# One transformer layer on one core: expert weights stored with even columns first, three stages run without borders between blocks, and the state-space setup staged a turn ahead

## The chip, the cores and the metric

The kernel runs on one core of a Trainium2 chip. The metric is the device time of one execution in microseconds; several executions are taken, and their median stands for the kernel.

## The reference, cut to what matters

One decoder layer with 1024 positions of width 1024, everything in fp32. A token mixer (a state-space branch beside dilated window attention) is followed by a residual and a LayerNorm, then by a mixture of 64 small experts, 8 of them for each position, and a shared one, and by a second residual and LayerNorm.

```python
def token_mixer(x, w_in, b_in, ...):
    proj = x @ w_in + b_in
    u, q, k, v, g_ssm, g_attn = jnp.split(proj, SPLIT_POINTS, axis=-1)
    y_ssm = s5_branch(u, lam_re, lam_im, log_dt, b_re, b_im, c_re, c_im, d_skip, w_glu) @ w_br_ssm
...
    merged = jax.nn.sigmoid(g_ssm) * y_ssm + jax.nn.sigmoid(g_attn) * y_attn
    return merged @ w_out

def swiglu(x, w_gate, w_up, w_down):
    return (jax.nn.silu(x @ w_gate) * (x @ w_up)) @ w_down
...
    def expert_block(acc, blk):
        e, rows, g = blk
        yb = swiglu(x2[rows], w_gate[e], w_up[e], w_down[e])
        return acc.at[rows].add(yb * g[:, None].astype(x2.dtype)), None
```

An expert has gate and up weights of 1024 x 256 and down weights of 256 x 1024, 3 MB together in fp32. The state-space branch (`s5_branch`) has 32 groups of 16 channels with 64 complex states each.

## The kernel before, in words

The program is a row of blocks. In each block every engine has its own stream of instructions, ordered by semaphores, and at a block's end all engines wait for each other; the setup of a block's semaphores and buffers stands there too. The blocks that matter here are these.

**`mixer_input`** transposes x, projects u (`ps_u`), works out the parameters of the state-space branch, and ends in a loop of TURNS = 8 turns over four groups each:

- ScalarE's `order` copies four groups of u (`u_tok`) into the buffer `u_stage`, in runs of 16 floats. VectorE's `stage` forms four products `w_prod` (L666) and combines them into `w_stage` (L672). Both buffers are single; `stage` of turn it waits for `turned`, the end of the transposes of the turn before.
- TensorE waits for `staged` and `ordered`, transposes four pieces of `u_stage` (L529) and four of `w_stage` (L531) into PSUM, makes the response products `ps_k` (L538, 16 instructions), waits for the copies of the transposes, and makes the states `ps_v` (L548, 16 instructions).
- ScalarE waits for `turned`, runs `order` for the next turn, copies the transposes into `ut_stage` (L602) and `wt_stage`, and then the responses into `k_resp`.
- GpSimd copies `ut_stage` on into `ut_all` (L473; the trace shows `ut_all` as part of `merged`). VectorE's `keep_states` copies `ps_v` into `keep["states"]`, behind `stage` of the next turn.

**`attention`** begins on TensorE with 16 steps of projection (`pe_project`, from L90, `mm3`: three fp32r products of high and low parts for one fp32 product). The first four steps fill one PSUM bank (`ps_p[:, 0]`), the fifth begins the second, where the states of the setup stood. Later lines that the rows show are L1239, L1040 and L1014, products of the attention's end with operands that lie next to each other.

**`project_and_route`** makes the output projection, LayerNorm, the router and the shared expert, whose last `down` on TensorE and `add_share` on VectorE end the block. It also asks for the first experts' weights and for the rows of the first items.

**`experts`** works on a list of 66 items, each a run of up to 160 positions of one expert. They are sorted by count into width classes, WIDTHS = (160, 144, 128, 112, 96); in the traced execution 12 items have width 160, 24 have 144, 14 have 128, 10 have 112 and 6 have 96. One turn does one item; the turns go in pairs with two sets of buffers (j = 0, 1). On TensorE a turn is: sums for the index of the item after next (L1816, L1818); 64 gate and up instructions (L2600: 2 matrices, 2 column halves c, 8 pieces k of the inner dimension; each fp32 product is two instructions in the trace); `turn_rows`, the transposes of the next item's rows (L2579, L2584); at widths over 128 the remaining rows' down product (L2614); and the down product as `mm3` (L90 to L92). The weights' stationary operand of L2600 is

```python
w3(raw[j][w])[:, k, c:2 * P:2]
```

that is, 128 columns, every second float of a run of 256, because hidden unit 2p + c is to stand on partition p: the down weights are loaded with two neighbouring rows on one partition. ScalarE makes, in this order, the high part of the next item's down weights (`split_hi`, L2642), SiLU, half of the next rows' copies, and the outputs. VectorE makes the low part of the down weights (`split_lo`, L2693) behind each piece of the high part, and the hidden values (`hidden`). SyncE asks for the weights of the item two turns ahead, with one transfer of 1024 KB for each of gate, up and down, when the buffers of the set come free. GpSimd gathers the rows of an item from `scr_x` (L1792) and adds the outputs to `scr_acc` (L2556). Ahead of the loop, TensorE runs `turn_rows(0)`; ScalarE runs `rows_in(0)` and `split_hi(0)`, and in its first turn `split_hi(1)` before item 0's SiLU.

Of the kernel before, what the change touches and what calls it, by code (L numbers as in the profile page):

```python
# [23 lines left out]
P = 128  # L24
D = 1024
# [277 lines left out]
def mixer_input(nc, m, cst, io, xT_hi, xT_lo, keep, scr, first):  # L303
# [5 lines left out]
    with ExitStack() as stack:  # L309
# [30 lines left out]
        ut_stage = a.sb("ut_stage", [P, 4, P])  # L340
# [6 lines left out]
        ld_x = [a.sem(f"ld_x{j}") for j in range(NT)]  # L347
        ld_dt, dt_ready, ld_lam, lam_copied = (a.sem(n) for n in ("ld_dt", "dt_ready", "ld_lam", "lam_copied"))
        ld_w = [a.sem(f"ld_uw{j}") for j in range(RAW)]
        ld_par, ld_bias = a.sem("ld_par"), a.sem("ld_bias")  # L350
        x_turned, x_hi_made, x_lo_made = a.sem("x_turned"), a.sem("x_hi_made"), a.sem("x_lo_made")
        p_turned, p_copied = a.sem("p_turned"), a.sem("p_copied")
        w_hi_made, w_lo_made, w_used = a.sem("uw_hi_made"), a.sem("uw_lo_made"), a.sem("uw_used")
        u_done, u_evac = a.sem("u_done"), a.sem("u_evac")
        den_ready, rden_ready, fac_ready, pow_ready, par_ready = (a.sem(n) for n in ("den_ready", "rden_ready", "fac_ready", "pow_ready", "par_ready"))
        pool_ch, dve_ch = a.sem("mi_pool_ch"), a.sem("mi_dve_ch")
        cpow_ready, zero_ready = a.sem("cpow_ready"), a.sem("zero_ready")
        ordered = a.sem("s5_ordered")
        staged, turned, copied_u, copied_w = a.sem("s5_staged"), a.sem("s5_turned"), a.sem("s5_ut"), a.sem("s5_wt")
        k_done, k_copied, v_done, v_copied = a.sem("s5_k"), a.sem("s5_kc"), a.sem("s5_v"), a.sem("s5_vc")  # L360
        ut_kept, stored, kd_ready = a.sem("s5_ut_kept"), a.sem("mi_stored"), a.sem("kd_ready")
# [5 lines left out]
        ps_ut = ps_u[:, 0].rearrange("p a (b c) -> p (a b) c", b=2)  # L367
        ps_wt = ps_u[:, 1].rearrange("p a (b c) -> p a b c", b=2)
# [48 lines left out]
        with nc.Block() as block:  # L417
            @block.sync
            def _(sp):
                def load_w(n):  # L420
                    if n >= RAW:
                        sp.wait_ge(w_lo_made, n - RAW + 1)
                    sp.dma_start(w_raw[:, n % RAW, :], w_d[:, n % KD, 0:SSM_W]).then_inc(ld_w[n % RAW], 16)

                for s in range(NT):
                    sp.dma_start(x_tok[:, s, :], x_d[:, s, :]).then_inc(ld_x[s], 16)
                    if 2 <= s < 2 + RAW:
                        load_w(s - 2)
                for n in range(RAW, 2 * RAW - 1):
                    load_w(n)  # L430
                for j, n in enumerate(("ssm_b_re", "ssm_b_im")):
                    sp.dma_start(b_raw[:, j, :, :], io[n][0].rearrange("(a g) n c -> (g n) a c", g=2)).then_inc(ld_par, 16)
                for j, n in enumerate(("ssm_c_re", "ssm_c_im")):
                    for half in range(2):
                        for g in range(2):
                            sp.dma_start(c_rows[:, j, half, SSM_N * g:SSM_N * g + SSM_N],
                                         io[n][0, 16 * half + g:16 * half + 16:2].rearrange("a c n -> a c n")).then_inc(ld_par, 16)
                sp.dma_start(d_row[:, :, :], io["ssm_d"].rearrange("o g c -> o (g c)").broadcast_to((SSM_C, SSM_G * SSM_C))
                             .rearrange("p (g c) -> p g c", c=SSM_C)).then_inc(ld_par, 16)
                sp.dma_start(bias_u[:, :], b_row[:, 0:SSM_W].broadcast_to((P, SSM_W))).then_inc(ld_bias, 16)  # L440
                for n in range(2 * RAW - 1, 2 * KD):
                    load_w(n)
                sp.wait_ge(w_lo_made, 2 * KD)
                first.load(sp)

                sp.wait_ge(zero_ready, 1)
                sp.dma_start(scr["k_pad"][:, :, 0:KP0], zeros[0:SSM_C, 0:KP0].unsqueeze(1).broadcast_to((SSM_C, SSM_G, KP0))).then_inc(stored, 16)
                for g2 in range(2):
                    rows = slice(64 * g2, 64 * g2 + 64)
                    sp.dma_start(scr["c_op"][rows, :, P * (1 - g2):P * (1 - g2) + P], zeros[rows, :].unsqueeze(1).broadcast_to((64, 2 * PAIRS, P))  # L450
                                 ).then_inc(stored, 16)
                sp.wait_ge(cpow_ready, 1)
                for g2 in range(2):
                    rows = slice(64 * g2, 64 * g2 + 64)
                    sp.dma_start(scr["c_op"][rows, :, P * g2:P * g2 + P],
                                 c_pow[rows, :, :, 1:T + 1, :].rearrange("p r a t c -> p (r a) (t c)")).then_inc(stored, 16)
# [20 lines left out]
            def _(pe):  # L477
# [22 lines left out]
                for n in range(2 * KD):  # L500
# [5 lines left out]
                    for s in range(4 * half, 4 * half + 4):  # L506
                        if half and k == 0:
                            pe.wait_ge(u_evac, s - 3)
# [2378 lines left out]
```

## Time and profile before

| what | value |
|---|---|
| median of 3 runs | 2113.94 us (2113.0 to 2120.82) |
| profiled execution | 2118.44 us, its span 2116.7 us |
| mean clock granted to TensorE | 0.977 |
| TensorE (PE) busy | 1997.8 us, 94% |
| its weight loads (PEld) | 1735.7 us, 82% |
| VectorE (DVE), ScalarE (ACT), GpSimd (POOL) busy | 1132.1, 771.5, 540.9 us |
| gate and up products, L2600 | 4224 instructions, 536.3 us |
| data moved | 390.19 MB, mean 184 GB/s |

The profiled execution is another one than the three timed runs; its own time lies 4.5 us above their median. The span is what the rows are placed in, in microseconds from its start. The setup loop runs up to 112 us, the attention block follows, and the experts' loop stands from about 1224 to 2084 us. TensorE is busy nearly all the time, so its share says little: whether it runs at its own pace, and where it stands still, has to be read from single stretches.

### The profile page before, as it was taken

The numbers are of one execution on the slowest core, as the hardware profiler recorded it, in microseconds if no ns is written. First come the engines' busy times: TensorE is split into PE (matmuls) and PEld (weight loads), VectorE is DVE, ScalarE is ACT, GpSimd is POOL, SyncE is SP. The second block draws the span as 40 slices with busy tenths as digits, with TensorE's granted clock in tenths as the row PEclk, the third lists the DMA queues.
The fourth block names the chain that finished last, engine by engine and source line by source line (L and its number), as shares of the span: only waits on it lengthen the run. The fifth ranks groups of instructions, "written<-read, shape, count | busy, mean of one in ns | idle before, by whom it ended". The sixth has DMA issues, their size and how long they took to land. (4 is left out here: it accounts for less than half of the span.)

```text
span 2116.7 us, 39190 instructions
## 1 busy us (share of the span) xinstructions
PE 1997.8 (94%) x12849; PEld 1735.7 (82%) x12849; DVE 1132.1 (53%) x3379; ACT 771.5 (36%) x1517; POOL 540.9 (26%) x969
## 2 busy tenths in 40 slices
PE   7889999999999889999899989999999999999992
PEld 7768889888988778888687778898888889999991
DVE  5833664456356652222556755555555556666654
ACT  4322453355144431111434023333333333333334
POOL 7145555200022300000100223334444332222120
PEclk9999999999999999999999999999999999999996
DMA  5522132211234521110341489999999999999995
GB/s 165 129 50 75 46 86 66 65 46 46 70 109 125 139 60 41 49 55 5 125 158 67 161 294 319 313 307 314 317 321 325 316 312 369 371 356 339 345 342 174
DMA packets 181200, 390.19 MB, mean 184 GB/s; under 512 B 26553, under 2 KB 121149, under 8 KB 155510
## 3 DMA queue, kind: packets, MB, share of 16 engines
q1 hardware_dynamic: 155568, 317.52, 41.7%
q0 software_dynamic: 25376, 71.46, 15.3%
q8 instruction: 52, 0.85, 0.2%
q14 instruction: 38, 0.31, 0.0%
q10 hardware_dynamic: 166, 0.05, 0.0%
HBM read 330.94 MB, written 64.98 MB: 187 GB/s over the span
## 5 line engine op out<-in xcount | busy, mean ns | idle before, releaser
L2600 PE MATMUL ps_gu<-xe,w_raw 128*128 128x144 f32 (+4 forms) x4224 | 536.3, 288 | 0.0
L2600 PEld LDWEIGHTS ps_gu<-xe,w_raw 128*128 128x128 f32 x4224 | 524.8, 197 | 0.2
L2642 ACT ACTIVATE w_hi<-w_raw 128x1024 fp32r<-128x1024 f32 x132 | 132.1, 1048 | 161.5 <-DMA w_raw<-in_exp_w_down 161.5
L2693 DVE TENSOR_TENSOR w_lo<-w_raw,w_hi 128x1024 fp32r<-128x1024 f32 x132 | 155.5, 1218 | 64.4 <-ACT w_hi L2642 64.3
L2556 POOL DMA_INDIRECT scr_acc<-y_main,out_idx x66 | 102.5, 1553 | 309.1 <-ACT y_main L2671 288.8
L1141 ACT ACTIVATE w_raw_first<-w_raw_first,o_stage 128x128 f32<-128x128 f32 (+1 forms) x192 | 86.4, 450 | 200.1 <-DVE o_stage L1089 199.2
L2671 ACT ACTIVATE y_main<-ps_ye,gate 128x512 f32<-128x512 f32 (+2 forms) x132 | 90.8, 688 | 123.5 <-PE ps_ye L92 123.5
L2647 ACT ACTIVATE xe<-ps_gu 128x512 f32<-128x512 f32 (+2 forms) x66 | 38.4, 581 | 216.2 <-PE ps_gu L2579 216.2
L2551 POOL DMA_INDIRECT scr_acc<-y_rest,out_idx x36 | 58.2, 1617 | 226.3 <-ACT y_rest L2668 226.3
L90 PE MATMUL ps_ye<-w_hi,e_h_hi 128*128 128x512 f32 (+2 forms) x264 | 109.9, 416 | 0.8 <-DVE e_h_lo L2720 0.7
L1808 DVE TENSOR_SCALAR e_sel<-e_slots,e_place 128x256 bf16<-128x256 bf16 (+1 forms) x536 | 104.6, 272 | 0.0
L92 PE MATMUL ps_ye<-w_hi,e_h_lo 128*128 128x512 f32 (+2 forms) x264 | 103.5, 392 | 0.0
L91 PE MATMUL ps_ye<-w_lo,e_h_hi 128*128 128x512 f32 (+2 forms) x264 | 103.4, 392 | 0.0
L1792 POOL DMA_INDIRECT x_main<-scr_x,idx x66 | 73.1, 1107 | 77.0 <-issue 47.9
L1827 DVE TENSOR_TENSOR e_idx_f<-ps_xt,e_neg_slot 128x2 f32<-128x2 f32 x64 | 10.2, 159 | 147.6 <-PE ps_xt L1818 122.2
L1040 PEld LDWEIGHTS ps_mixer<-merged,w_raw_first 128*128 128x128 f32 x560 | 78.4, 193 | 10.2 <-ACT w_raw_first L1150 1.7
L1040 PE MATMUL ps_mixer<-merged,w_raw_first 128*128 128x64 f32 x560 | 85.7, 261 | 1.1 <-DVE w_raw_first L1097 1.1
L90 PE MATMUL ps_mixer<-v_w_hi,xT_hi 128*128 128x512 f32 x192 | 80.5, 419 | 6.1 <-DVE v_w_lo L860 4.0
L90 PE MATMUL ps_mixer<-xT_hi,w_hi_first 128*128 128x512 f32 x192 | 79.4, 414 | 5.2 <-PEq L105 5.2
L1102 DVE COPY o_stage<-ps_mixer 128x64 f32<-128x64 f32 x192 | 42.4, 221 | 76.5 <-PE ps_mixer L1040 76.2
L1299 POOL TENSOR_TENSOR o_stage<-o_stage,att_wts 128x512 f32<-128x512 f32 x8 | 8.8, 1098 | 289.4 <-DVE att_wts L1289 289.4
L860 DVE TENSOR_TENSOR v_w_lo<-v_w_raw,v_w_hi 128x512 fp32r<-128x512 f32 x48 | 33.6, 702 | 87.4 <-ACT v_w_hi L856 87.3
(460 smaller groups left out, 4774.3 us busy)
## 6 DMA issues: line engine op xcount, KB each, us to landing
w_raw<-in_exp_w_gate SPq DMA_DIRECT2D x66, 1024.0 KB, 8.2
w_raw<-in_exp_w_up SPq DMA_DIRECT2D x66, 1024.0 KB, 7.4
w_raw<-in_exp_w_down SPq DMA_DIRECT2D x66, 1024.0 KB, 8.1
w_raw_first<-in_w_in SPq DMA_DIRECT2D x24, 512.0 KB, 4.4
v_w_raw<-in_w_in SPq DMA_DIRECT2D x48, 256.0 KB, 2.7
merged<-in_x SPq DMA_DIRECT2D x14, 512.0 KB, 5.0
scr_att<-o_stage SPq DMA_DIRECT2D x16, 264.0 KB, 3.0
att_prev<-scr_att SPq DMA_DIRECT2D x16, 264.0 KB, 3.4
```

Source lines behind the costliest of these rows:

```text
L90: eng.matmul(out, lh, rh, start=first, stop=False, skip_group_check=True)
L91: eng.matmul(out, lh, rl, start=False, stop=False, skip_group_check=True)
L92: return eng.matmul(out, ll, rh, start=False, stop=last, skip_group_check=True)
L1040: ins = pe.matmul(ps_o[:, w % 2, 0:DH], probs_T[:, w % 2, P * j:P * j + P], v_cur[:, kb, P * hp + DH * h2:P * hp + DH * h2 + DH], start=(j ...
L1141: act.activation(probs[:, w % 2, 0:n], probs[:, w % 2, 0:n], ACT.Exp, scale=-1.0, bias=o_stage[:, blk, at + 1:at + 2], accum_out=o_stage[: ...
L1792: pool.indirect_dma_start(out=self.x_main[j][0:rows, :], out_offset=None, in_=self.x_rows[0], in_offset=bass.IndirectOffsetOnAxis(ap=self. ...
L1808: ins = dve.tensor_scalar(self.sel[:, s, 0:slots], self.slots[:, 0:slots], self.place[:, s:s + 1], None, ALU.is_equal)
L2556: pool.indirect_dma_start(out=acc_rows[0], out_offset=bass.IndirectOffsetOnAxis(ap=out_idx[j][0:rows, 0:1], axis=0), in_=y_main[j][0:rows, ...
L2600: ins = pe.matmul(ps_gu[:, 2 * w + c, 0:width], w3(raw[j][w])[:, k, c:2 * P:2], xT[:, k, 0:width], start=(k == 0), stop=(k == KD - 1))
L2642: act.activation(piece_of(hi[j], piece), piece_of(raw[j][DOWN], piece), ACT.Copy).then_inc(hi_made, 1)
L2671: act.activation(y_main[j][0:rows, 512 * half:512 * half + 512], ps_y[0:rows, half, :], ACT.Copy, scale=gate[j][0:rows, 0:1]).then_inc(y_e ...
L2693: tt(piece_of(lo[j], piece), piece_of(raw[j][DOWN], piece), piece_of(hi[j], piece).bitcast(F32), ALU.subtract).then_inc(lo_made, 1)
```

## The change

Four edits. Most of the diff's length is indentation; it is shown here without it.

**Expert weights.** Before the launch, the host stores the columns of `exp_w_gate` and `exp_w_up` with the 128 even ones first and the 128 odd ones behind them. The kernel reads half c as a run of 128 neighbouring columns.

```diff
     for name, value in inputs.items():
         arr = np.ascontiguousarray(value)
+        if name in ("exp_w_gate", "exp_w_up"):
+            arr = np.ascontiguousarray(arr.reshape(1, NE, D, P, 2).swapaxes(3, 4)).reshape(arr.shape)
...
-                                ins = pe.matmul(ps_gu[:, 2 * w + c, 0:width], w3(raw[j][w])[:, k, c:2 * P:2], xT[:, k, 0:width],
+                                ins = pe.matmul(ps_gu[:, 2 * w + c, 0:width], w3(raw[j][w])[:, k, P * c:P * c + P], xT[:, k, 0:width],
                                                 start=(k == 0), stop=(k == KD - 1))
```

**The border before the attention.** `mixer_input` no longer has a block. It returns one function for each engine, and the attention block calls them at its head. Its semaphores come from the outer memory `m`. At their ends GpSimd, ScalarE and VectorE wait for the setup's stores, and GpSimd and VectorE for the last states too; TensorE waits for the states ahead of its fifth projection step.

```diff
-        with nc.Block() as block:
-            @block.sync
-            def _(sp):
+        def opening_sync(sp):
...
+            pool.wait_ge(ordered, TURNS)
+            pool.wait_ge(k_done, TURNS)
+            pool.wait_ge(v_copied, TURNS)
+            pool.wait_ge(stored, 16 * 5)
...
+            dve.wait_ge(stored, 16 * 5)
+            dve.wait_ge(v_copied, TURNS)
+
+        return opening_sync, opening_tensor, opening_scalar, opening_vector, opening_pool
...
             def _(sp):
+                opening_sync(sp)
                 sp_load_bias(sp, 0)
...
             def _(pe):
+                opening_tensor(pe)
                 for step in range(16):
+                    if step == 4:
+                        pe.wait_ge(first.states_kept, SSM_G // 4)
                     pe_project(pe, step, 0)
```

**The border before the experts.** `project_and_route` likewise returns `routing_sync` and its four sisters, which the experts' block calls at the head of each engine's stream.

```diff
             def _(pe):
+                routing_tensor(pe)
+
                 def turn_rows(j, uses, width):
...
+                pe.wait_ge(it.shares, NT - 1)
+                pe.wait_ge(it.idx_made, 2)
                 turn_rows(0, 1, CAP)
+                pe.wait_ge(it.shares, NT)
                 kinds, rest_pairs, pairs = classes(pe)
```

**The setup loop.** TensorE transposes turn it + 1 before it does the products of turn it, with two PSUM targets in turn. ScalarE copies the transposed u straight into `ut_all`; `ut_stage` and GpSimd's copy are gone. `order` moves from ScalarE to GpSimd, `keep_states` from VectorE to ScalarE, and ScalarE's and GpSimd's loops are written out.

```diff
-        ps_ut = ps_u[:, 0].rearrange("p a (b c) -> p (a b) c", b=2)
-        ps_wt = ps_u[:, 1].rearrange("p a (b c) -> p a b c", b=2)
+        ps_ut = [ps_u[:, 0].rearrange("p a (b c) -> p (a b) c", b=2), ps_x[:, 2, :].rearrange("p (g c) -> p g c", g=4)]
+        ps_wt = [ps_u[:, 1].rearrange("p a (b c) -> p a b c", b=2), ps_x[:, 3, :].rearrange("p (a b c) -> p a b c", a=2, b=2)]
+        ut_of = lambda it: keep["ut_all"][:, 512 * it:512 * it + 512].rearrange("p (g c) -> p g c", g=4)
...
-                with pool.Fori(0, TURNS) as it:
-                    pool.wait_ge(copied_u, it + 1)
-                    pool.tensor_copy(keep["ut_all"][:, bass.ds(it * 512, 512)],
-                                     ut_stage[:, :, :].rearrange("p a b -> p (a b)")).then_inc(ut_kept, 1)
+            for it in range(TURNS):
+                if it == 0:
+                    pool.wait_ge(u_evac, NT)
+                else:
+                    pool.wait_ge(turned, it)
+                pool.tensor_copy(u_stage[:, :, :].rearrange("p g (s c) -> p g s c", s=T),
+                                 u_tok[:, :, 64 * it:64 * it + 64].rearrange("p s (g c) -> p g s c", g=4)).then_inc(ordered, 1)
...
-                for it in range(TURNS):
+            def turn_stage(it):
                     pe.wait_ge(staged, it + 1)
                     pe.wait_ge(ordered, it + 1)
+                if it >= 2:
+                    pe.wait_ge(copied_w, it - 1)
                     for g in range(4):
-                        pe.transpose(ps_ut[:, g, :], u_stage[:, g, :], ident[:, :])
+                    pe.transpose(ps_ut[it % 2][:, g, :], u_stage[:, g, :], ident[:, :])
                     for j in range(4):
-                        ins = pe.transpose(ps_wt[:, j // 2, j % 2, :], w_stage[:, j // 2, j % 2, :], ident[:, :])
+                    ins = pe.transpose(ps_wt[it % 2][:, j // 2, j % 2, :], w_stage[:, j // 2, j % 2, :], ident[:, :])
                     ins.then_inc(turned, 1)
+
+            turn_stage(0)
+            for it in range(TURNS):
+                if it + 1 < TURNS:
+                    turn_stage(it + 1)
+                if it:
                     pe.wait_ge(k_copied, it)
...
+            def keep_states(it):
+                act.wait_ge(v_done, it + 1)
+                act.activation(keep["states"][:, :, 2 * it:2 * it + 2, 1:NCH + 1],
+                               ps_v.rearrange("p a r k -> p r a k"), ACT.Copy).then_inc(v_copied, 1)
 
-                def responses(it, more):
+            def responses(it):
                     act.wait_ge(turned, it + 1)
-                    if more:
-                        order(it + 1)
-                    act.wait_ge(ut_kept, it)
-                    act.wait_ge(v_done, it)
-                    act.activation(ut_stage[:, :, :], ps_ut, ACT.Copy).then_inc(copied_u, 1)
-                    act.activation(wt_stage[:, :, :, :], ps_wt, ACT.Copy).then_inc(copied_w, 1)
+                act.activation(ut_of(it), ps_ut[it % 2], ACT.Copy).then_inc(copied_u, 1)
+                if it:
+                    keep_states(it - 1)
+                act.activation(wt_stage[:, :, :, :], ps_wt[it % 2], ACT.Copy).then_inc(copied_w, 1)
                     act.wait_ge(k_done, it + 1)
```

## Rows read from the trace of the kernel before

**Rows 1.** Timeline, TensorE, gate and up streams of three turns: start, length (us), instructions
```profile
1706.63 8.09 PE L2600 MATMUL ps_gu<-xe,w_raw 128*128 128x144 f32 x64
...
1792.38 7.78 PE L2600 MATMUL ps_gu<-xe,w_raw 128*128 128x128 f32 x64
...
2020.64 7.76 PE L2600 MATMUL ps_gu<-xe,w_raw 128*128 128x96 f32 x64
```

**Rows 2.** Timeline, TensorE and its weight loads, 596.4 to 597.6 us
```profile
596.63 0.61 PE L1239 MATMUL ps_mixer<-v_w_raw,merged 128*128 128x128 f32 x4
...
597.07 0.30 PEld L1040 LDWEIGHTS ps_mixer<-merged,w_raw_first 128*128 128x128 f32 x2
...
597.29 0.19 PEld L1014 LDWEIGHTS ps_mixer<-k_two,q_two 128*128 128x128 f32 x1
```

**Rows 3.** Windows: us, busy PE PEld DVE ACT POOL, clock, DMA share, GB/s
```profile
1758.00:1884.00 126.00, 126.00 (x1021) 118.71 (x1017) 79.80 (x309) 47.48 (x78) 30.97 (x22) 1.00 1.02 366
1906.00:1998.00 92.00, 92.00 (x749) 84.65 (x747) 56.22 (x224) 34.12 (x58) 20.30 (x16) 1.00 1.03 342
```

**Rows 4.** DMA issues in the turns from 1758.0, 1884.0, 1895.4, 1998.0: us to landing
```profile
w_raw<-in_exp_w_down SPq DMA_DIRECT2D x1, 1024.0 KB, 8.7
...
w_raw<-in_exp_w_down SPq DMA_DIRECT2D x1, 1024.0 KB, 8.0
...
w_raw<-in_exp_w_down SPq DMA_DIRECT2D x1, 1024.0 KB, 10.7
...
w_raw<-in_exp_w_down SPq DMA_DIRECT2D x1, 1024.0 KB, 17.5
```

**Rows 5.** Waits of ScalarE, 2009 to 2056 us: us, times, longest
```profile
ACT w_hi L2642 <- DMA w_raw<-in_exp_w_down: 10.9, 4, 3.7
```

**Rows 6.** Timeline and windows at the border before the attention
```profile
111.18 1.09 PE L548 MATMUL ps_u<-ut_stage,wt_stage 128*64 128x128 f32 x16 [0.23 <-issue]
...
117.52 0.77 PE L90 MATMUL ps_mixer<-xT_hi,w_hi_first 128*128 128x512 f32 x1 [5.25 <-PEq L105]
...
116.00:123.00 7.00, 5.48 (x13) 4.37 (x14) 2.16 (x2) 1.06 (x1) 4.52 (x7) 0.51 0.73 142
123.00:130.00 7.00, 7.00 (x31) 5.69 (x31) 1.50 (x2) 1.37 (x2) 3.58 (x15) 1.00 0.04 11
```

**Rows 7.** Timeline at the border before the experts, all engines
```profile
1227.73 1.94 PE L2579 MATMUL ps_gu<-ident,x_main 128*128 128x128 f32 x8 [5.80 <-PEq L105]
...
1235.31 2.00 ACT L2642 ACTIVATE w_hi<-w_raw 128x1024 fp32r<-128x1024 f32 x2 [2.90 <-DMA w_raw<-in_exp_w_down]
...
1239.93 2.35 DVE L2693 TENSOR_TENSOR w_lo<-w_raw,w_hi 128x1024 fp32r<-128x1024 f32 x2
...
1243.89 1.07 PE L2614 MATMUL ps_ye<-w_raw,e_h 128*32 128x256 f32 x16
```

**Rows 8.** Groups by form, TensorE, L2600: busy us, mean ns | idle before
```profile
L2600 PE MATMUL ps_gu<-xe,w_raw 128*128 128x128 f32 x896 | 109.0, 283 | 0.0
L2600 PE MATMUL ps_gu<-xe,w_raw 128*128 128x112 f32 x640 | 77.7, 283 | 0.0
L2600 PE MATMUL ps_gu<-xe,w_raw 128*128 128x96 f32 x384 | 46.4, 282 | 0.0
```

**Rows 9.** Timeline of the setup loop, all engines, from 101 us
```profile
101.44 0.60 PE L531 MATMUL ps_u<-ident,w_stage 128*128 128x128 f32 x4
...
102.30 0.42 DVE L666 TENSOR_TENSOR w_prod<-s_rpow_re,b_bar 128x256 f32 x1 [0.41 <-PE ps_u L531]
...
103.46 0.74 POOL L473 COPY merged<-ut_stage 128x512 f32 x1 [3.22 <-ACT ut_stage L602]
...
104.40 0.41 DVE L672 TENSOR_TENSOR w_stage<-w_prod 128x256 f32<-128x256 f32 x1
104.91 0.66 PE L529 MATMUL ps_u<-ident,u_stage 128*128 128x128 f32 x4
...
105.40 0.60 PE L531 MATMUL ps_u<-ident,w_stage 128*128 128x128 f32 x4
105.93 1.06 PE L538 MATMUL ps_x<-c_pow,b_bar 64*16 64x128 f32 x16
```

More of the change, by code:

```diff
@@ L346, in mixer_input @@
         ps_u = a.ps("ps_u", [P, NT // 2, 2, 256])
[L347 to L359, printed above, removed]
@@ L360, in mixer_input @@
-        k_done, k_copied, v_done, v_copied = a.sem("s5_k"), a.sem("s5_kc"), a.sem("s5_v"), a.sem("s5_vc")
-        ut_kept, stored, kd_ready = a.sem("s5_ut_kept"), a.sem("mi_stored"), a.sem("kd_ready")
+        ld_x = [m.sem(f"ld_x{j}") for j in range(NT)]
+        ld_dt, dt_ready, ld_lam, lam_copied = (m.sem(n) for n in ("ld_dt", "dt_ready", "ld_lam", "lam_copied"))
+        ld_w = [m.sem(f"ld_uw{j}") for j in range(RAW)]
+        ld_par, ld_bias = m.sem("ld_par"), m.sem("ld_bias")
+        x_turned, x_hi_made, x_lo_made = m.sem("x_turned"), m.sem("x_hi_made"), m.sem("x_lo_made")
@@ L362, in mixer_input @@
+        ordered = m.sem("s5_ordered")
+        staged, turned, copied_u, copied_w = m.sem("s5_staged"), m.sem("s5_turned"), m.sem("s5_ut"), m.sem("s5_wt")
+        k_done, k_copied, v_done, v_copied = m.sem("s5_k"), m.sem("s5_kc"), m.sem("s5_v"), m.sem("s5_vc")
+        stored, kd_ready = m.sem("mi_stored"), m.sem("kd_ready")
+        first.states_kept = v_copied
         ident = cst["ident"]
@@ new lines, in opening_pool @@
+        def opening_pool(pool):
+            cst["write"](pool)
+            pool.memset(zeros[:, :], 0.0).then_inc(zero_ready, 1)
+            pool.wait_ge(lam_copied, 4)
+            t = {"raw": lam_raw, "scratch": scratch, "bits": bits, "rden": rden,
+                 "den_ready": den_ready, "rden_ready": rden_ready,
+                 "fac_ready": fac_ready, "pow_ready": pow_ready, "wide": [scratch_w[:, n, :] for n in range(4)]}
+            s5_parameters(pool, pool_ch, t, par)
+            pool.sem_inc(par_ready, 1)
+            for it in range(TURNS):
[9 more added lines that the diff above has]
+            pool.wait_ge(stored, 16 * 5)
@@ L731, in at, with attention @@
             return t.sb(name, shape, dt)
-def attention(nc, m, cst, io, xT_hi, xT_lo, keep, scr, first, late, merged):
+def attention(nc, m, cst, io, xT_hi, xT_lo, keep, scr, first, late, merged, opening):
     with ExitStack() as stack:
         a = Memory(nc, stack)
+        opening_sync, opening_tensor, opening_scalar, opening_vector, opening_pool = opening
         RAW, WR = 3, 2
@@ L1643, in _ @@
             def _(act):
+                opening_scalar(act)
                 act_split(act, 1)
@@ L1686, in _ @@
             def _(pool):
+                opening_pool(pool)
                 for j in range(2):
```

1411 lines of the change are left out of this document (698 added, 713 removed).

## The prediction, made before the changed kernel was run

> **What bounds the kernel now.** Two questions: does PE run at its own pace in the experts' loop, which is 40% of the span, and where does it stand still at the borders of blocks?
>
> For the first I took the timeline, one turn for each width [rows 1]. A turn's 64 gate and up matmuls (each fp32 product is two instructions) take 8.09 us at width 144, 7.78 at 128 and 7.76 at 96. Without the last matmul's own 0.28 us, over 63 steps, that is 124 ns, then 119 ns and 119 ns. Below 144 the moving columns shrink and the step does not: something else sets it, and what is left is the load of 128 stationary columns, every second float of a partition's line. Loads of neighbouring floats, fp32 as well, go faster [rows 2]: the four products of L1239 take 0.61 us, (0.61 - 0.27)/3 = 113 ns, and the two loads of L1040 and the one of L1014 behind them start at 597.07 to 597.29, 0.11 us apart, though the matmuls between have only 64 columns. So the strided load costs some 9 ns a matmul where the width is 128 or less.
>
> Then the windows by stage and the DMA view, because a shorter turn asks for the same 3 MB of weights sooner. In the stages of width 128 and 112 the DMA share is 1.02 and 1.03, with PE busy all the time [rows 3]: the DMA engines are full too. The landing time of the down weights shows how near the edge they are [rows 4]: 8.7 us at the start of the stage of 128, 8.0 in its last turn, 10.7 in the first turn of width 112, and 17.5 nine turns on. A backlog grows by (17.5 - 10.7)/9 = 0.76 us a turn while PE keeps its 11.4 us. At width 112 a turn's transfers take longer than PE's turn; PE does not feel it only because loads are asked for well over a turn ahead. In the next stage, of 96, ScalarE does wait for them, 10.9 us in four turns [rows 5]: there the room ends.
>
> For the second question, the timeline at the borders: PE stands 5.25 us before L90 at 117.52 [rows 6] and 5.80 us before L2579 at 1227.73 [rows 7], in both cases for the barrier.
>
> **The change, part by part.**
>
> *Neighbouring columns.* In 14 turns of width 128, 10 of 112 and 6 of 96 (896, 640 and 384 matmuls [rows 8]) the step should fall from 119 to about 109.5 ns: 1920 x 9.5 ns = 18.2 us of PE's stream. At 144 the step of 124 ns is set by the columns, more than a contiguous load needs, so nothing is had there, nor at 160. No transfer changes size: a partition's line stays 8 KB.
> What of the 18.2 us is kept is decided by the DMA engines. PE's turn falls by 0.61 us, at 128 from 11.45 to 10.84. At 128 the engines move 366 GB/s x 11.45 us = 4.19 MB a turn [rows 3], and the landing time sinks from 8.7 to 8.0 over eleven turns, so their own turn is a little under PE's: I put it at 11.2 us, an estimate. Over 14 turns at 10.84 the landing time grows by 14 x 0.36 = 5 us, to 13. It jumps by 2.7 at the step to 112, as now (8.0 to 10.7), and is then at 15.7; the room ends at 17 to 18. So one or two turns later PE goes at the DMA's pace, about 11.9 us (11.4 and half a microsecond; the 0.76 is of the last of the three loads). Sum: 14 x -0.61 = -8.5; 1.5 x -0.61 = -0.9; 8.5 x +0.5 = +4.2; at 96 nothing, since PE already waits there; the last two turns, which load nothing, -1.2. Together **-6.4 us**. Bounds: -2 (engines full from width 128 on, only the tail shrinks) and -18.2.
> One rule of the Trainium skill speaks against this part. Rows first: contiguous 110 to 113 ns, stride two 119 ns [rows 1, 2]. The page "Advanced Engine Details and Errata", section Memory Cachelines, has lines of 16 bytes and full speed when at least two accesses hit a line; at a stride of two floats two do. By that rule this part gives 0 and the whole change -9.2 us; by the rows it gives -6.4 and the whole -15.6.
>
> *First border.* The projection's first four steps use a bank that nothing holds; the fifth waits for the last states, which ScalarE copies while PE is in those four steps. So the whole hole goes: -5.25 us. The clock was granted at 0.51 in 116 to 123, where 13 products took 5.48 us; right behind, at full clock, 31 took 7.00 us, 0.226 each [rows 6]. With no hole ahead I expect full clock: 5.48 - 13 x 0.226 = -2.5 us. If the clock falls all the same, this is 0.
>
> *Setup a turn ahead.* The cycle now is not PE's. The transposes end at 102.04, DVE's `stage` runs from 102.30 to 104.81, the next transposes start at 104.91 [rows 9]; the next stage waits for them, since `w_stage` is one buffer. That loop (the transposes of 101.44 stand again at 105.40, 3.96 us) is left as it is: `stage` still waits for `turned`, the transposes for `staged`. PE's hole ahead of L548 lies inside it. DVE sheds its copy of the states, which ran while it waited. POOL's `order` replaces POOL's copy (0.74 us [rows 9]) and starts with `stage`; its price is unknown: at least that 0.74 of the same size, at most about 2 us if runs of 16 floats cost threefold. Queued behind it are only the transposes, and it has 2.5 us; I take 0.8. So the middle turns keep their time. At the ends: the first period, PE-bound at half clock, gets about one set of L538 shorter, -0.9, as products move behind the second transposes; after the last transposes two sets of L538 and of L548 remain instead of one (1.06 and 1.09 us each, somewhat less in a row) [rows 6, 9], +1.9. Net **+1.0 us**, bounds -1 and +3. First border and setup together: **-6.75 us**.
>
> *Second border.* `turn_rows(0)` can follow the last `down` at once, so PE is up to 5.8 us earlier. But ScalarE splits item 1's down weights before it makes item 0's SiLU, and those are issued behind the last store in both kernels. They land at 1235.3; ScalarE waits 2.90 us for them even now [rows 7]. Their two pieces end at 1237.3; DVE's w_lo, which now ends at 1242.28, can end one piece (1.18) behind, at 1238.5, and L2614 comes 1.6 behind that, as now: 1240.1 instead of 1243.89, -3.7. New transfers now fall beside that load: two gathers, some 0.65 MB at 366 GB/s, 1.8 us, of which I take two thirds. **-2.5 us**, bounds -1 and -7.
>
> Sum: -6.4 - 6.75 - 2.5 = -15.65 us. The profiled execution took 2118.44 (span 2116.7), and would take 2102.8; the median of the three runs, 2113.94, becomes **2098.3**. Half a per cent, about which a measurement can decide, is 10.6 us: faster means below 2103.4.
>
> **The rivals.**
> 1. *The DMA engines follow.* A share of 1.0 is partly packets stretched by one another, and more outstanding loads are served faster. For it: 366 GB/s at 128 beside 342 at 112, so the rate is no constant [rows 3]. Against it: the backlog at 112, which grows although loads are always outstanding. The first part then gives -18.2, the whole -27.4: 2086.5.
> 2. *The first part gives 0 to 2 us*, by the rule above or because transfers are the whole bound from width 128 on: -9.2 to -11.2, 2103 to 2105. For it: a DMA share of 1.02 in the stage of 128. Against it: the step of 119 ns.
> 3. *The borders give little*: the clock falls elsewhere, item 1's weights land later still, `order` disturbs DVE. Borders -3, first part -6.4: 2104.5.
> 4. *Slower: POOL's `order` becomes the setup's cycle.* Up to 2.5 us it is hidden; each microsecond above costs 8. To eat 15.65 us it must take 2.5 + 1.96 = 4.5 us, six times the present copy; to end 10.6 us slower, 5.8 us. At 6 us: -15.65 + 28 = +12.3, 2126. For it: only the unknown pattern; against it: 0.74 us for as many floats.
>
> **How the numbers follow.** Forecast as summed, 0.52; rival 1, 0.17; rival 2, 0.15; rival 3, 0.12; rival 4, 0.04. Faster: the forecast, rival 1 and about a third of rivals 2 and 3, whose times lie at the bound, 0.78. Same: the rest of them, 0.18. Slower: 0.04. The forecast's own range is 2092 to 2103. The range that holds 8 in 10 goes from 2085, which takes in rival 1 at full size, to 2106, which takes in rivals 2 and 3.
>
> **What would show it.** In the profile after: a 128-wide stream of 7.2 us instead of 7.78; if it still reads 7.78, rule and rival 2 are right. Turns of 10.84 us at width 128 with down weights landing later and later, then turns of 11.8 to 12 us with waits of PE at 112; if turns stay at 10.8 to the end, rival 1. A setup cycle of 3.96 us, with `order` under 2.5 us. No hole of 5 us near 113 and full clock behind it. A wait of PE for SiLU of 2 to 4 us in the experts' first turn; if there is none, the second border gives near 6. The prediction is wrong if the DMA's own turn at width 128 is not near 11.2 us, on which 12 us hang, or if PE's clock falls in a new place.

## The result, and the profile after

Over 20 runs of each kernel the median went from 2113.88 to 2104.46 us. The ratio to the kernel before is 0.9949, with a 95% interval of 0.9937 to 0.996: by it 10.8 us less, between 8.5 and 13.3; the two medians themselves are 9.4 us apart. The prediction was 2098.3, in a range of 2085 to 2106. The profiled execution took 2110.43 us (span 2108.7), one of the longer ones; its span is 8.0 us shorter than that of before.

The trace after, in the order of rows 1 to 9. First the gate and up streams of three turns on TensorE, widths 128, 112 and 96 (timeline: start, length):

```profile
1821.72 7.39 PE L2616 MATMUL ps_gu<-xe,w_raw 128*128 128x128 f32 x64
...
1943.18 7.38 PE L2616 MATMUL ps_gu<-xe,w_raw 128*128 128x112 f32 x64
...
2013.18 7.36 PE L2616 MATMUL ps_gu<-xe,w_raw 128*128 128x96 f32 x64
```

A stream of width 128 is 0.39 us shorter than in [rows 1]. The step from one product to the next is (7.39 - 0.28)/63 = 113 ns. At width 144 the busy time of the group is 194.1 us beside 194.3 before: nothing, as forecast.

Windows of the stage of 128, of the last five turns of width 112, and of two turns of 96:

```profile
1821.70:1888.20 66.50, 66.50 (x560) 62.41 (x556) 43.17 (x166) 25.91 (x43) 15.96 (x12) 1.00 1.03 376
1943.20:2001.60 58.40, 56.30 (x463) 50.38 (x460) 35.03 (x142) 21.11 (x35) 12.67 (x10) 1.00 1.03 347
2013.10:2036.50 23.40, 22.33 (x194) 19.78 (x190) 13.89 (x58) 8.33 (x15) 4.96 (x4) 1.00 1.02 343
```

And the waits of TensorE (1730 to 2070) and of ScalarE (1943.2 to 2048): us in total, times, longest.

```profile
PE ps_ye L90 <- DVE e_h_lo L2742: 5.2, 11, 0.8
...
ACT w_hi L2663 <- DMA w_raw<-in_exp_w_down: 27.4, 8, 4.0
```

At width 128 a turn takes 66.5/6 = 11.08 us, without a gap. At 112 the five turns take 58.4/5 = 11.7, of which TensorE is busy 11.26. In TensorE's row VectorE is named as the engine waited for, which works off the low part of the weights first; it gets those from ScalarE, and ScalarE waited for the down weights, 27.4 us in eight turns. Read both rows together: the second says where the first comes from.

The first border, timeline and windows, to be read beside [rows 6]:

```profile
112.85 1.09 PE L561 MATMUL ps_u<-merged,wt_stage 128*64 128x128 f32 x16 [0.24 <-issue]
113.87 0.50 PE L90 MATMUL ps_mixer<-xT_hi,w_hi_first 128*128 128x512 f32 x1
...
116.00:123.00 7.00, 7.00 (x31) 5.68 (x31) 2.28 (x3) 1.37 (x2) 4.88 (x12) 1.00 0.71 150
```

The hole is gone and the granted clock is 1.00 (2.4 GHz) in 116 to 123, where it was 0.51 (about 1.2 GHz). One turn of the setup, all engines, beside [rows 9]:

```profile
93.40 0.60 PE L537 MATMUL ps_x<-ident,w_stage 128*128 128x128 f32 x4
...
94.07 0.62 POOL L474 COPY u_stage<-merged 128x512 f32<-128x512 f32 x1 [3.28 <-PE ps_x L537]
94.27 0.69 DVE L674 TENSOR_TENSOR w_prod<-s_rpow_re,b_bar 128x256 f32 x1 [1.41 <-PE ps_x L537]
...
96.34 0.42 DVE L680 TENSOR_TENSOR w_stage<-w_prod 128x256 f32<-128x256 f32 x1
...
97.30 0.60 PE L537 MATMUL ps_u<-ident,w_stage 128*128 128x128 f32 x4
```

The cycle is 3.90 us, VectorE and the transposes one after the other as before; GpSimd's `order` takes 0.62.

The second border, timeline and one row of TensorE's waits, beside [rows 7]:

```profile
1219.98 1.03 PE L2595 MATMUL ps_gu<-ident,x_main 128*128 128x128 f32 x8
...
1227.24 11.14 PE L2616 MATMUL ps_gu<-xe,w_raw 128*128 128x160 f32 x64
...
1233.78 2.00 ACT L2663 ACTIVATE w_hi<-w_raw 128x1024 fp32r<-128x1024 f32 x2 [10.23 <-DMA w_raw<-in_exp_w_down]
...
1239.40 1.07 PE L2630 MATMUL ps_ye<-w_raw,e_h 128*32 128x256 f32 x16
...
PE ps_xt L1828 <- issue: 5.6, 1, 5.6
```

The transposes start 7.75 us sooner, and most of that goes into a new hole of 5.6 us behind them. The program has TensorE wait there for the last share, whose addition ends at 1222.15, and then load the five loop bounds. The down product of the rest (L2630) starts 4.49 us sooner than L2614 did; 1.4 us of each of these two figures is the lead that the kernel has when it comes to this stage.

The same points in both traces, from the timeline, give the lead of the changed kernel, that is, by how many us it is ahead there:

| point | before | after | lead |
|---|---|---|---|
| first projection product | 117.5 | 113.9 | 3.6 |
| 14th projection product | 123.1 | 117.0 | 6.1 |
| in the shared expert, last product of the sums L1818 (L1830 after) | 1206.6 | 1205.2 | 1.4 |
| second item's first gate product | 1248.2 | 1243.7 | 4.5 |
| first item of width 128 | 1734.3 | 1730.2 | 4.1 |
| last product | 2076.2 | 2067.7 | 8.5 |
| end of the span | 2116.7 | 2108.7 | 8.0 |

Three gains (6.1, 3.1 and 4.4 us; the experiments separate them) stand in it, and a loss of 4.7 between 123 and 1206 us, where the diff touches next to nothing.

### The profile page after: what moved, and what is told of

Same layout as the page of the kernel before. It is cut to its first block and busy times, and to the rows that moved or that the text cites. A ratio compares the mean times of both kernels' runs of the same rounds, so it can differ in the third digit from the quotient of the medians.

```text
span 2108.7 us, 39053 instructions
## 1 busy us (share of the span) xinstructions
PE 1988.2 (94%) x12849; PEld 1722.0 (82%) x12849; DVE 1125.3 (53%) x3371; ACT 771.8 (37%) x1517; POOL 536.2 (25%) x969
## 5 line engine op out<-in xcount | busy, mean ns | idle before, releaser
L2616 PE MATMUL ps_gu<-xe,w_raw 128*128 128x144 f32 (+4 forms) x4224 | 524.8, 285 | 0.0
L2616 PEld LDWEIGHTS ps_gu<-xe,w_raw 128*128 128x128 f32 x4224 | 513.1, 191 | 0.2
L866 DVE TENSOR_TENSOR v_w_lo<-v_w_raw,v_w_hi 128x512 fp32r<-128x512 f32 x48 | 33.7, 703 | 88.6 <-ACT v_w_hi L862 88.6
```

The source lines that it names most:

```text
L2616: ins = pe.matmul(ps_gu[:, 2 * w + c, 0:width], w3(raw[j][w])[:, k, P * c:P * c + P], xT[:, k, 0:width], start=(k == 0), stop=(k == KD - 1))
```

## The experiments

On the chip of the next four kernels the kernel before had a median of 2117.58, in the second four 2115.92, in the last 2117.28. Times are compared by their ratios to it; 0.9949 (0.9937 to 0.996) is the changed kernel's, from another chip. Most parts are worth 2 to 6 us of 2100, so two intervals often overlap, and then only the stretches of the traces tell the kernels apart. By "the stretch" is meant that from the first product of width 128 to the last product.

**1. One part undone at a time.** First the layout.

```diff
-  w3(raw[j][w])[:, k, P * c:P * c + P]
+  w3(raw[j][w])[:, k, c:2 * P:2]
```

> The changed kernel with the expert weights as before: even and odd columns interleaved, the stationary operand every second float. My theory (a strided load sets the step below width 144; the DMA engines take back most of it): the 128-wide stream of 64 goes from 7.39 back to 7.78 us, the middle turns of width 128 from 11.07 to 11.45; the stretch from the first 128-wide turn to the last product, 337.9 us in the changed kernel, becomes 342 (4 us longer), and the time 2108.5. Rival, the DMA engines follow the stream everywhere and the lost part lies elsewhere: 11 to 12 us longer, 2116. Rival, the layout gives nothing in time: the stretch stays within 1 us.

Measured: 2110.57, ratio 0.9971 (0.9957 to 0.9984); the interval just overlaps the changed kernel's. The streams of 128 are 7.78 us again. Windows of the stretch, first this kernel, then the changed one:

```profile
1728.30:2070.50 342.20, 341.52 (x2735) 316.45 (x2732) 204.94 (x802) 125.44 (x207) 75.45 (x59) 1.00 0.99 340
```
```profile
1730.20:2068.00 337.80, 332.56 (x2734) 304.09 (x2730) 203.70 (x802) 125.39 (x207) 75.55 (x59) 1.00 1.00 346
```

The stretch differs by 4.4 us, as expected. TensorE's busy time falls by 9.0: half of what it saves comes back as waiting (337.80 - 332.56 = 5.2 in place of 342.20 - 341.52 = 0.7).

The border before the attention, its functions in a block of their own:

```diff
-        return opening_sync, opening_tensor, opening_scalar, opening_vector, opening_pool
+        with nc.Block() as block:
+            @block.tensor
+            def _(pe):
+                opening_tensor(pe)
...
+        return [lambda eng: None] * 5
```

> The changed kernel with a block of its own around the opening again, its end a barrier ahead of the attention; the setup loop stays a turn ahead. My theory: a hole of about 5.3 us comes back ahead of the first projection product, and TensorE's granted clock falls to half behind it, 2 to 2.5 us more over the first 13 products; 7 to 7.5 us longer at 125 us of the span. Over the whole kernel, if the lead is kept to the end: 2111.5. Rival: the lead is eaten by stretches of half clock that come at other times whatever the start was (in the two profiles a lead of 5.85 us at 123 us was 1.5 us at 1210): the time is then 2104 to 2107.

Measured: 2108.58, ratio 0.9954 (0.9936 to 0.9972), not to be told from the changed kernel. The expected times are on the scale of the first chip (2113.88 before): there the ratio gives 2104.2, the rival's time, and the theory's 2111.5 is outside the interval. In the trace the first product stands at 116.39:

```profile
116.39 0.77 PE L90 MATMUL ps_mixer<-xT_hi,w_hi_first 128*128 128x512 f32 x1 [2.06 <-PEq L698]
...
116.00:123.00 7.00, 6.61 (x22) 5.35 (x23) 2.17 (x2) 1.06 (x1) 4.99 (x9) 0.76 0.77 150
```

The hole is 2.06 us and not the 5.3 expected. Half clock is back behind it (0.76 on average in the window): the 13 products take 4.6 us in place of 3.1. The 14th comes at 121.0, 4.0 later than without the border; the setup ends 0.4 later in this execution. So 3.6 to 4.0 of the 6.1 us are the border's. Where the rest comes from is read from the traces and was not tried by itself. The semaphores moved to the outer memory, and VectorE's queue is shorter: in the kernel before, the split of the first weights and k_resp's end stand behind the last states, the store of k_resp is issued at 115.46, and TensorE goes on 2.06 us later; here the issue is at 115.09 and TensorE follows 1.30 later.

The border before the experts, in the same way:

> The changed kernel with a block of its own around projection and routing again, its end a barrier ahead of the experts. My theory: the hole ahead of the first item's transposes comes back (5.8 us), the one ahead of the sums (5.6 us now) shrinks to 1.7, and the second turn's gate and up products start 3 us later against the last shared product: 2107.5. Rival: the landing of the second item's down weights sets the first turn in both, and the time moves by under 1 us.

Measured: 2108.8, ratio 0.9958 (0.9942 to 0.9975). The hole ahead of the transposes is 5.1 us, the one behind them 1.7 again:

```profile
PE ps_gu L2616 <- PEq L2441: 5.1, 1, 5.1
...
PE ps_xt L1828 <- issue: 1.7, 1, 1.7
```

The second item's gate products start at 1246.6, 41.6 us behind the point in the shared expert (1205.0), as in the kernel before (41.6); in the changed kernel it is 38.5. The border cost 3.1 us, as expected; by time the two kernels' intervals overlap. ScalarE's and VectorE's rows for the second item's down weights say how, first of this kernel, then of the changed one:

```profile
1233.91 2.00 ACT L2684 ACTIVATE w_hi<-w_raw 128x1024 fp32r<-128x1024 f32 x2 [3.73 <-DMA w_raw<-in_exp_w_down]
...
1237.68 2.35 DVE L2736 TENSOR_TENSOR w_lo<-w_raw,w_hi 128x1024 fp32r<-128x1024 f32 x2
```
```profile
1234.87 2.36 DVE L2715 TENSOR_TENSOR w_lo<-w_raw,w_hi 128x1024 fp32r<-128x1024 f32 x2 [3.43 <-ACT w_hi L2663]
```

The weights land no sooner without the border: ScalarE begins on them 28.9 us behind the point in the shared expert here, 28.7 in the kernel before (1235.31) and 28.6 in the changed one (1233.78). What moves is VectorE's low part. With the border it begins 3.8 us behind the high part (4.6 in the kernel before), since VectorE is still at the index work of a later item (`e_sel`), which had started late; without it that work is done and the low part follows 1.09 us behind.

The setup loop of before, still without a border behind it:

```diff
-            turn_stage(0)
             for it in range(TURNS):
-                if it + 1 < TURNS:
-                    turn_stage(it + 1)
+                pe.wait_ge(staged, it + 1)
...
+                ut_stage[:, 2 * j + g2, :],
```

> The changed kernel with the setup loop of before (no transposes ahead, ut_stage and GpSimd's copy, order on ScalarE, keep_states on VectorE), still without a border behind it. My theory: the cycle is 3.96 us in place of 3.90, the first products start sooner, and the last state product ends 1 to 1.7 us sooner than in the changed kernel, so turning the setup a turn ahead cost about that: 2103. Rival: the products ahead hide the copies, and undoing it costs 1 us or more: 2105.5 or more.

Measured: 2104.14, ratio 0.9931 (0.9914 to 0.9948). The last state products start at 110.88, 1.97 us sooner than in the changed kernel, but the first projection product does not:

```profile
113.88 0.50 PE L90 MATMUL ps_mixer<-xT_hi,w_hi_first 128*128 128x512 f32 x1 [1.91 <-DVE w_lo_first L299]
```

It waits for VectorE's split of the first weights, queued behind `keep_states`. In the changed kernel VectorE has shed that copy and the split ends at 109.6. Both kernels stand at 113.9: the new setup loop costs TensorE about 2 us and spares it a wait of 1.9. Neither theory had this wait. By time the two kernels' intervals overlap.

**2. Are the DMA engines the limit of the narrow turns?** Half the bytes of the down weights (the rest of the buffer keeps old values), with both layouts:

```diff
+  if w == DOWN and width <= P:
+      sp.dma_start(raw[j][w][:, 0:D].unsqueeze(1), src[w][:, bass.ds(e, 1), 0:D]).then_inc(ld[j][w], 16)
```

> The changed kernel, but for experts of width 128 and less only half of the down weights is loaded (512 KB in place of 1024; the other half keeps stale values, so the output is not the reference's). My theory, the bytes of the weights set the pace from width 112 on: with 2.5 MB a turn the turns go at TensorE's own 11.07 us at width 128, 11.0 at 112 and 10.6 at 96 to the end, no wait for the low part of h or of the weights; the stretch from the first 128-wide turn to the last product shrinks from 337.5 us to about 329 (8 to 9 us less). Rival, the order of work on ScalarE and VectorE and not the bytes delays the down product at width 112: the turns of 11.5 to 12.1 us stay, and the stretch shrinks by under 2 us.

> As l1_light, with the weights laid out as before (every second float), so the layout's price is seen without the DMA engines' limit. My theory: 64 steps of 119 in place of 113 ns in each of 30 turns, 30 x 0.385 = 11.6 us more than l1_light in the stretch from the first 128-wide turn. Rival, that a stride of two floats costs nothing by itself: within 1 us of l1_light.

Measured: ratios 0.9926 and 0.9977 (0.9909 to 0.9942, 0.9962 to 0.9993). The same stretch, neighbouring columns first, then every second:

```profile
1726.60:2055.70 329.10, 328.91 (x2735) 304.69 (x2731) 202.88 (x802) 125.08 (x207) 77.20 (x59) 1.00 0.97 310
```
```profile
1727.60:2068.40 340.80, 340.61 (x2734) 316.50 (x2730) 204.76 (x802) 125.23 (x207) 77.25 (x59) 1.00 0.95 299
```

With room in the transfers the layout is worth 11.7 us (11.6 expected), and TensorE waits 0.2 us in all. The two intervals of time are clear of each other. So late weights are what takes the other 7 us away.

**3. Full, or slow?** The narrow classes left out, so that every item below 128 runs as 128:

```diff
-WIDTHS = (CAP, 144, P, 112, 96)
+WIDTHS = (CAP, 144, P)
```

> The changed kernel with three width classes in place of five (160, 144, 128): the items of widths 112 and 96 run as 128, with 128 rows gathered and added; nothing else changes. In the trace of the changed kernel the weights' packets of 8 KB took 311 ns each in the stage of 128 and 344 ns at 112. Theory a, the slower packets belong to the narrow turns' way of moving rows: with 128 rows the pace stays at TensorE's 11.07 us, no wait for late down weights after the first turns, and the stretch from the first 128-wide turn to the last product is 333 to 334 us in place of 337.5, the time 4 us less. Theory b, the engines are full and every byte costs: 0.13 to 0.26 MB more a turn at 347 GB/s is 0.4 to 0.75 us in each of 16 turns, and the stretch grows by 4 to 8 us.

Measured: 2101.3, ratio 0.993 (0.9913 to 0.9948). Two windows over later turns, up to the last but one:

```profile
1880.50:1991.20 110.70, 110.70 (x925) 103.89 (x923) 71.48 (x280) 43.01 (x71) 26.53 (x20) 1.00 1.03 369
1991.20:2035.30 44.10, 44.10 (x367) 41.42 (x364) 28.24 (x112) 17.32 (x28) 10.63 (x8) 1.00 1.02 363
```

They hold ten and four turns, 11.07 and 11.03 us each, without a wait. The stretch is 332.2 us, 5.6 less than with the narrow widths, although more bytes are moved: 369 GB/s against 347. By time the interval still overlaps the changed kernel's a little, but the traces repeat it: five other kernels with the changed kernel's code in the stretch took 336.0 to 340.9 us there, and the one of point 4 that has this edit too took 332.4. The share of the DMA engines is 1.03 in both, so it can't tell full from slow. The Trainium skill, "Perfetto Trace Analysis", section Identifying the Most-Contended Engine, says so: for DMA look at how far the memory's bandwidth is used and not at the occupancy, which 16 engines make misleading. Here the trace agrees: 1.03 at 347 and at 376 GB/s. The packets themselves show it: in the changed kernel one of 8 KB takes 311 ns on average in the turns of 128, some 345 in those of 112 and 352 in those of 96; in this kernel it is 312 to the end. What makes them slower while 112 or 96 rows are gathered and added was not found; gather and addition were not tried apart.

**4. The cycle of the setup.** `u_stage` and `w_stage` twice; `stage` and `order` wait for the transposes of two turns before. VectorE's loop is written out as well.

```diff
+        u_stage = [u_stage, a.sb("u_stage_2", [P, 4, P])]
+        w_stage = [w_stage, a.sb("w_stage_2", [P, 2, 2, P])]
...
-                    dve.wait_ge(turned, it)
+                    dve.wait_ge(turned, it - 1)
```

> The changed kernel with u_stage and w_stage twice, so that VectorE stages turn it while TensorE still holds the buffer of turn it - 1. My theory, the cycle of the setup (3.90 us) is VectorE's five to six operations and the transposes one after the other over a single buffer: it falls to TensorE's own 3.2 us (8 transposes and 32 products), the last state product starts at 108 to 109.5 us in place of 112.85, and the time falls by 3 to 5 us if the lead is kept: 2103 against a changed kernel of 2106.8 on this chip. Rival, ScalarE's four copies and their handing on set the cycle: it stays at 3.9 us, and nothing changes.

Measured: 2097.57, ratio 0.9913 (0.9898 to 0.9928), clear of the changed kernel: 0.0036 less, 7.6 us, where 3 to 5 were expected. Timeline:

```profile
97.14 0.60 PE L539 MATMUL ps_u<-ident,w_stage 128*128 128x128 f32 x4
...
100.18 0.60 PE L539 MATMUL ps_x<-ident,w_stage 128*128 128x128 f32 x4
...
105.05 0.50 PE L90 MATMUL ps_mixer<-xT_hi,w_hi_first 128*128 128x512 f32 x1
```

The cycle is 3.04 us, TensorE no longer waits in it, and the first product comes 8.8 us sooner. The last five of the seven periods give 5 x 0.86 = 4.3 of it. The first two give 3.8 (2.08 and 3.49 us in place of 4.77 and 4.57), since the second turn is staged while TensorE is still at the first. The remaining 0.7 is the execution's own: its first transposes stand that much sooner. The writing out of the loop is not the gain, since a turn of `stage` takes 2.6 us here and 2.5 in the changed kernel.

With the three widths as well:

> As t1_twice, with the three width classes of w1_wide. Whatever w1_wide shows in the stretch is added to the time of t1_twice (0.9913 of the kernel before): 0.989 by theory a, 0.994 by theory b.

Measured: 2095.46, ratio 0.99 (0.9882 to 0.9918), the lowest here, though the interval overlaps that of the double buffers alone. The first projection product stands at 106.73. From the first transposes to it are 26.2 us here, 25.6 with the double buffers alone and 33.7 in the changed kernel, so the second buffer is worth 7.5 to 8.1 us at this point.

**5. The new hole at the second border.** The five loads ahead of the transposes:

```diff
+                kinds, rest_pairs, pairs = classes(pe)
                 turn_rows(0, 1, CAP)
                 pe.wait_ge(it.shares, NT)
-                kinds, rest_pairs, pairs = classes(pe)
```

> The changed kernel with TensorE's five loads of the loop bounds moved ahead of the first item's transposes. My theory: they make the hole of 5.6 us ahead of the first sums together with the wait for the last share; ahead of the transposes they stand behind the same earlier wait, so the hole falls to 2 to 3 us while the transposes come up to 3 us later. ScalarE waits for the second item's down weights 10.2 us in the first turn, and these land when they land: the second turn's gate and up products start at most 1 us sooner, and the time stays within noise. Rival, the hole is paid for in full: 3 us less.

Measured: 2105.89, ratio 0.9959 (0.9946 to 0.9973): no gain. The transposes come at 1222.67 behind a hole of 4.0 us, where 2 to 3 were expected, and ScalarE still waits 7.38 us for the second item's down weights. This run moves the hole and does not take it away, and the weights came later in it: ScalarE begins on them 31.5 us behind the point in the shared expert (28.6 in the changed kernel), and the second item's gate products start 40.4 behind it (38.5). So it doesn't tell what the hole costs. A row of the changed kernel does, roughly:

```profile
1238.51 0.32 DVE L2738 TENSOR_TENSOR e_h<-e_silu,ps_gu 128x160 f32<-128x160 f32 x1 [0.46 <-PE ps_gu L2616]
```

VectorE makes the second half of item 0's hidden values here. It waits 0.46 us for the gate and up products that the hole delayed; all it did before hangs on the weights that ScalarE got at 1233.78. An estimate from this row is that the hole costs some half a microsecond.

**6. The layout alone, and stride four.** The kernel before with the first edit only.

> The kernel before with the first edit alone: even columns first, neighbouring columns read. My theory: the edit is worth the same without the others, 4.3 us in the stretch from the first 128-wide turn to the last product (341.9 to 337.6), and 0.998 of the kernel before. Rival: with the earlier start of the experts gone, the backlog of the DMA engines differs and the stretch shrinks by less than 2 or more than 6 us.

Measured: 2113.0, ratio 0.9976 (0.9963 to 0.9989), clear of 1. The stretch is 337.0 us, 5.3 less than before (342.3), within 1 us of what it is worth in the whole change. This run bears on something else too. Windows from the 14th projection product to the last product of the sums in the shared expert, of before, of the changed kernel, and of this one, whose code there is that of before:

```profile
123.10:1206.60 1083.50, 1047.31 (x5204) 878.32 (x5203) 540.49 (x1398) 389.84 (x862) 211.40 (x592) 0.99 0.25 76
```
```profile
117.00:1205.20 1088.20, 1050.59 (x5205) 880.21 (x5204) 540.80 (x1398) 389.88 (x862) 214.88 (x597) 0.98 0.26 76
```
```profile
121.90:1211.70 1089.80, 1051.16 (x5203) 880.39 (x5202) 540.63 (x1398) 390.02 (x862) 211.53 (x593) 0.98 0.25 76
```

1083.5 and 1089.8 us for the same work, at a mean clock of 0.99 and 0.98. Cut into 57 windows each, the granted clock adds up to some 27 us at half clock in the kernel before, and to some 38 in both the changed kernel and this one. The other ten profiles of the changed kernel's family took 1084.8 to 1092.0 us. So the loss of 4.7 us between the two profiles is of the size by which executions of the same code differ, and nothing speaks for the change as its cause; the profile of before was a quick one in this part.

Then the changed kernel with the stationary operand read at every fourth float:

> The changed kernel with the stationary operand of the gate and up products read at every fourth float over a double run (it holds the wrong columns, so the output is not the reference's). Two rivals on what sets the load's time. One, the time grows with the line count: 113 ns at stride one, 119 at stride two, and at stride four far more, near the 311 ns that loads at stride four take elsewhere in the trace of before, so a 128-wide stream of 64 takes 12 to 20 us. Two, the price of 6 ns at stride two is one of the pattern as such: stride four costs the same 119 ns, 7.8 us a stream.

Measured in one run of 2580.18 us, one stream of width 128:

```profile
2116.85 15.18 PE L2616 MATMUL ps_gu<-xe,w_raw 128*128 128x128 f32 x64
```

At a mean of 398 ns an instruction that is (15.18 - 0.40)/63 = 235 ns a step. So the series is 113, 119, 235 ns at strides of one, two and four floats: the first rival, at less than the 311 ns it named.

## Why the prediction was right

The time lies in the stated range, but 2104.46 is outside the forecast's own part of it (2092 to 2103) and just where rivals 2 (2103 to 2105) and 3 (2104.5) stood. The time alone can't tell them apart. The traces do: the step fell and the first part gave 4.4 us, where rival 2 gave it 0 to 2, and the borders with the setup gave 9.2 us in the profiles, where rival 3 gave them 3. Point by point, by the prediction's own steps:

**Neighbouring columns: the mechanism right, two sizes off.** The step fell to 113 ns, not to 109.5. [Rows 2] had both prices: 113 for four products of 128 columns, 110 for loads beside products of 64; the prediction took the lower one, for products that are wider. 30 turns x 0.39 = 11.7 us of TensorE's stream were saved, where 18.2 were forecast. The sum was less wrong than its terms, and that was luck: 4.4 us in the profiles (5.3 in the kernel with this edit alone) for 6.4, presumably since a turn that shrank less also ran less far ahead of its weights. At width 128 the prediction gave the DMA engines a turn of 11.2 us; but for three turns of 11.4 to 12.1 near its start they kept 11.07 through the stage. At 112 it forecast 11.9 after one or two turns and got 11.7 after five turns at 11.0. By step the series is 113, 119 and 235 ns. The rule of the Trainium skill that spoke for 0 (the page "Advanced Engine Details and Errata", section Memory Cachelines: two hits on a line of 16 bytes are enough) does not hold in full: with two floats a line the step is 6 ns longer, though with one it doubles, which fits the line.

**The engines are full.** This reading of [rows 3] and [rows 4] is the step that failed. The backlog at 112 was real, and half the bytes did away with it; but it came from a slower rate in the narrow turns (347 GB/s) and not from an upper limit on bytes: with 128 rows the engines moved 369 GB/s in the same turns and nothing waited. The rate of 366 beside 342 GB/s in the same rows showed it, and the prediction used it only for rival 1. Rival 1 was right for width 128 and wrong for the rest.

**First border and setup.** Forecast 5.25 + 2.5 - 1.0 = 6.75, measured 6.1 at the 14th product. The hole went whole. Full clock was granted, worth 2.5: the 13 products took 3.1 us in place of 5.6. The setup's cost was 1.67 us at the last state products (forecast 1.0), inside its bounds. What the prediction missed is that the hole was not the barrier's alone (with the border back it is 2.06 us, not 5.3), and that without the setup's edit TensorE would have waited 1.9 us for VectorE. The cycle itself stayed, 3.90 us for 3.96, for the reason given: one buffer. `order` took 0.62 us for the 0.8 assumed, so rival 4 had no ground.

**Second border.** Forecast 2.5, measured 3.1. It was decided as said at the second item's down weights, by VectorE's low part: 3.7 us was forecast for that, less 1.2 for weights that land later beside new transfers. They did not: ScalarE begins on them 28.6 us behind the point in the shared expert, 28.7 before. The wait of TensorE was forecast in the first turn for SiLU, with a gain near 6 us if there was none. There was none, and the gain was 3.1: the wait stands ahead of the first sums instead, 5.6 us. The loads of the loop bounds that fall into it were not in the prediction.

**The sum.** In the profiles it is 6.1 + 3.1 + 4.4 = 13.6 us in the parts that the change touches, 15.65 forecast; by time it is 10.8, and 13.3 is the interval's end. Some of the 13.6 may be given back in the middle, where executions differ by more than that; how much stays open.

## What to carry to other kernels

A busy share of 1.0 on the DMA engines does not say that they are full: look at the GB/s beside it, and if it is lower than in another stage, ask what that stage does differently before bytes are saved. When a loop's cycle goes round through a buffer that one engine fills and another empties, look at the buffer before the order of work: a second one gave 7.5 to 8.1 us at the first product here, on top of the turn ahead, which had given nothing by itself. The second buffer without the turn ahead was not run. And when a border is taken away, read who would have been late without it; the wait behind it is often another engine's queue.

## What the runs showed of the hardware

A stationary fp32 operand of 128 columns is loaded at a pace of 113 ns a product when its floats are neighbours, 119 ns at every second, 235 ns at every fourth (moving operands of 128 columns). Weight packets of 8 KB took 311 ns in turns that gather and add 128 rows and some 345 ns in turns of 112 rows (376 against 347 GB/s, the engines' share 1.03 in both). The same instructions over 1083.5 us took 1089.8 in another execution, with TensorE's mean clock at 0.98 for 0.99; a difference of 6 us between two profiles of this kernel carries no meaning unless it is placed in a stretch at clock 1.00.
